# Two weight sums moved from VectorE to GpSimd, and a weight split issued one tile earlier, in a decoder layer's feed-forward part

## The reference

```python
def conv_ffn(h, prefix, w_up, conv_w, conv_b, w_down):
    up = h @ w_up                                        # 1024 -> 2 x 2816
    c, new_state = causal_dwconv(up, prefix, conv_w, conv_b)   # 3 taps along the tokens
    g, u = c[..., :D_FF], c[..., D_FF:]
    return (jax.nn.silu(g) * u) @ w_down, new_state      # 2816 -> 1024
```

## Time and profile before

| | |
|---|---|
| median of 3 runs | 877.42 us (877.25 to 877.79) |
| the profiled execution | 876.97 us, of which the span of the trace is 875.1 |
| PE busy | 850.4 us, 97% of the span |
| DVE busy | 554.5 us, 63% |
| ACT busy | 363.6 us, 42% |
| POOL busy | 68.8 us, 8% |
| granted TensorE clock, mean | 0.996 |
| the feed-forward part | from about 470 us to the end |

### The profile page before, as it was taken

One profiled execution on the slowest core, in us unless ns is written; L12 is line 12 of the kernel. 1 busy time (PEld: TensorE's weight loads), 2 busy tenths in 40 slices (PEclk: granted clock), 3 DMA queues, 4 the chain that ended last, 5 costly groups with the idle time before them and its releaser, 6 DMA issues.

```text
span 875.1 us, 17354 instructions
## 1 busy us (share of the span) xinstructions
PE 850.4 (97%) x6884; PEld 799.7 (91%) x6884; DVE 554.5 (63%) x981; ACT 363.6 (42%) x652; POOL 68.8 (8%) x149
## 2 busy tenths in 40 slices
PE   7999999999999999999999999999999999999995
PEld 7988878789999999877999999999999999999994
DVE  6344246677584732465455998778678696786754
ACT  7302133465553611354343754335244343452452
POOL 2320000000000000000000320100001001010200
PEclk9999999999999999999999999999999999999998
DMA  8798698731234555598233322232223322332222
GB/s 306 262 364 292 218 323 315 240 98 49 55 98 136 166 206 187 169 359 315 65 94 124 98 61 73 85 121 73 85 73 109 98 79 79 108 88 63 88 73 103
DMA packets 50146, 131.25 MB, mean 150 GB/s; under 512 B 5939, under 2 KB 8503, under 8 KB 49810
## 3 DMA queue, kind: packets, MB, share of 16 engines
q1 hardware_dynamic: 48064, 124.40, 43.1%
q0 software_dynamic: 1712, 5.62, 1.8%
q10 hardware_dynamic: 290, 0.12, 0.1%
HBM read 123.12 MB, written 7.00 MB: 149 GB/s over the span
## 4 chain that ended last, share of the span: by engine, by line
PE 69%; DVE 9%; ACT 4%; issue 3%; DVEq 0%; ACTq 0%
PE proj L1177 41%; PE proj L1133 3%; PE proj L1194 2%; PE proj L1196 2%; PE proj L1195 2%; DVE w_lo L1864 2%; PE score L1428 2%; PE score L1261 1%; PE score L1259 1%; PE score L1260 1%; PE T L1261 1%; PE T L1260 1%; PE T L1259 1%; PE score L1394 1%; DVE conv L2027 1%
## 5 line engine op out<-in xcount | busy, mean ns | idle before, releaser
L1177 PE MATMUL proj<-a_hi,w_hi 128*128 128x272 f32 (+1 forms) x740 | 160.7, 292 | 12.6 <-DVE w_lo L1864 6.3
L1528 ACT ACTIVATE w_hi<-w_raw 128x1024 fp32r<-128x1024 f32 (+2 forms) x128 | 119.0, 931 | 109.2 <-PE proj L1177 79.7
L1864 DVE TENSOR_TENSOR w_lo<-w_raw,w_hi 128x1024 fp32r<-128x1024 f32 (+2 forms) x128 | 136.9, 1070 | 34.7 <-ACT w_hi L1528 34.5
L1177 PE MATMUL proj<-a_lo,w_hi 128*128 128x272 f32 (+1 forms) x740 | 158.2, 288 | 0.0
L1177 PE MATMUL proj<-a_hi,w_lo 128*128 128x272 f32 (+1 forms) x740 | 158.0, 288 | 0.0
L1177 PEld LDWEIGHTS proj<-a_hi,w_hi 128*128 128x128 f32 x740 | 118.5, 189 | 20.9 <-DVE w_lo L1864 8.0
L1177 PEld LDWEIGHTS proj<-a_lo,w_hi 128*128 128x128 f32 x740 | 118.8, 189 | 0.0
L1177 PEld LDWEIGHTS proj<-a_hi,w_lo 128*128 128x128 f32 x740 | 118.4, 189 | 0.0
L1177 PE MATMUL proj<-d_hi,w_hi 128*128 128x272 f32 x448 | 92.4, 287 | 0.0
L1177 PE MATMUL proj<-d_lo,w_hi 128*128 128x272 f32 x448 | 92.1, 287 | 0.0
L1177 PE MATMUL proj<-d_hi,w_lo 128*128 128x272 f32 x448 | 92.1, 288 | 0.0
(11 more groups left out here) (360 smaller groups left out, 1653.0 us busy)
## 6 DMA issues: line engine op xcount, KB each, us to landing
w_raw<-in_w_up SPq DMA_DIRECT2D x28, 512.0 KB, 3.6
w_raw<-in_w_in SPq DMA_DIRECT2D x21, 512.0 KB, 3.9
early_pages<-in_cache_k SPq DMA_DIRECT2D x32, 256.0 KB, 6.2
pages<-in_cache_v SPq DMA_DIRECT2D x32, 256.0 KB, 5.3
c_pages<-in_cache_mem_k SPq DMA_DIRECT2D x16, 512.0 KB, 6.7
c_pages<-in_cache_mem_v SPq DMA_DIRECT2D x16, 512.0 KB, 5.8
p_raw<-in_w_up SPq DMA_DIRECT2D x16, 512.0 KB, 3.9
w_raw<-in_w_down SPq DMA_DIRECT2D x32, 256.0 KB, 2.6
```

The costliest lines, as they stand in the source:

```text
L1177: mm = pe.matmul(tile_banks(n)[:, half, 0:width], wt, act[:, at, half * HALF:half * HALF + width], start=(k == 0 and a == 0), stop=(k == w ...
L1528: act.activation(w_hi[:, n % W_HI_RING, 0:kt, :], w_raw[:, n % W_RING, 0:kt, :], ACT.Copy).then_inc(w_hi_ready, 1)
L1864: dve.tensor_tensor(w_lo[:, n % W_RING, 0:kt, :], w_raw[:, n % W_RING, 0:kt, :], w_hi[:, n % W_HI_RING, 0:kt, :].bitcast(F32), ALU.subtrac ...
```

## The change

Three edits. (1) In a plain column ahead of a paired one that has down tiles beside it, the splits of tile f + 3 (`w_hi` and `w_lo`) are issued in the step of the gate tile, right behind those of f + 2, and none in the step of the up tile. (2) GpSimd computes b12 - b11 and b22 - b12, with a wait of its own between the two. (3) DVE waits for both and computes the other two sums.

```diff
@@ make_schedule
         soon = PAIRED.index(i + 1) if i + 1 in PAIRED else None
         if not second and i == 0:
             s.append(("norm", "up"))
+        if soon is not None and beside_of(i):
+            after_hi, after_lo = split_next(f + 1)
+            hi, lo = ([], []) if second else (hi + after_hi, lo + after_lo)
         s += hi + [("up_in", i, int(second))] + lo
@@ the walk of GpSimd
+                if kind == "sums":
+                    for j in range(2):
+                        pool.wait_ge(sem(f"slot_landed1_{j}"), 16 * (PAGE_AREA.count(1) + arg + 1))
+                    if arg:
+                        wait_product(pool, arg - 1, 4)
+                    else:
+                        pool.wait_ge(sem("blend_lo"), 4)
+                    b11, b12, b22 = p_raw[:, 0, 0:4, :], p_raw[:, 1, 0:4, :], p_raw[:, 1, 4:8, :]
+                    pool.tensor_tensor(t_raw[:, 0, :, :], b12, b11, ALU.subtract).then_inc(sem("pool_sums"), 1)
+                    pool.wait_ge(sem("pool_sums"), 2 * arg + 1)
+                    pool.tensor_tensor(b12, b22, b12, ALU.subtract).then_inc(sem("pool_sums"), 1)
@@ the walk of VectorE, "sums"
                     one, two = slice(0, 4), slice(4, 8)
-                    b11, b21, b12, b22 = (p_raw[:, j, ks, :] for j in range(2) for ks in (one, two))
-                    side(dve.tensor_tensor(t_raw[:, 0, :, :], b12, b11, ALU.subtract))
-                    settle()
-                    side(dve.tensor_tensor(b12, b22, b12, ALU.subtract))
+                    b21, b22 = p_raw[:, 0, two, :], p_raw[:, 1, two, :]
+                    dve.wait_ge(sem("pool_sums"), 2 * arg + 2)
                     done(dve.tensor_tensor(t_raw[:, 1, :, :], t_raw[:, 0, :, :], b22, ALU.subtract))
                     dve.tensor_tensor(t_raw[:, 2, :, :], t_raw[:, 1, :, :], b21, ALU.add).then_inc(sem("sums_made"), 1)
```

## The result

| | before | after |
|---|---|---|
| median | 877.61 us of 4 runs (877.25 to 878.59) | 871.21 us of 4 runs (870.24 to 872.45) |
| ratio, 95% interval | | 0.992 (0.9907 to 0.9934) |
| the profiled execution, and its span | 876.97, 875.1 | 872.45, 870.7 |
| POOL busy | 68.8 us | 103.7 us |

The change is 0.8% faster, 6.4 us by the medians. I had forecast 877.3; the time lies just under my range. Two executions further down, one of the kernel before (1191.19 us) and one with pair 0's sums on VectorE (927.27 us), ran at a lower granted clock, and the ratios leave them out.

A forecast was written before the change was run, and what follows sets the result against it. The PE, busy 97% of the span, was taken as the bound, with 8.5 us of stalls to regain. Terms -5.6 + 3.6 + 1.9 = -0.1 on 876.97 gave 876.9, as a median 877.3 us; range 871.5 to 881.5.

The forecast's parts named there:

- the seven: PE stalls for w_lo at the second down tile of plain columns ahead of paired ones: 0.96 us each, 6.75 in all.
- The library load of 7.0 us: Column 4, ahead of GpSimd's first sum: a program library load, 6.3 plus 0.7 of issue; ends 0.3 and 10.
- the +3.6 of the wait: Column 4: VectorE waits for GpSimd behind the load, so the PE loses 5.4 us in place of 1.73.
- the +1.9 of the clock: Column 4: after a 5.3 us PE stop the clock falls to 1.2 GHz, about 19 matmuls 0.10 us longer.
- the rival of the cheap load: Column 4: library already there or in under 4 us; put at 872.4 us, chance 0.33.
- free form: Column 4, cheap load at no cost: stall 1.4 us, total -5.9, 871.5 us.
- -5.6 for seven pairs: Seven steady pairs: gain 0.8 us each, a 0.16 stall at the first down tile in place of 0.96.
- 1.2 us a sum: GpSimd's time per sum in the steady pairs, two streams and the fixed part; ends 0.5 and 1.6.
- the rival's 2.3 us stop: Column 4, cheap load of 3.9 us: the PE stands still 2.3 us, too short for the clock; total -5.0.
- no blocking: Steady pairs: GpSimd's sums don't block VectorE; the seven give 6.75, total 876.2 us, within the forecast's range.
- slow sums: Steady pairs: sums of 1.6 us each or more blocking, seven pairs give nothing; +5.5, 882.9 us, chance 0.09.
- the steady period of 276 matmuls: Sign in the steady pairs: about 34.7 us, 0.8 less than the 35.5 between two stalls before.

The follow-up runs named there:

- the split alone: Only the early split (w_hi and w_lo) put on the kernel before, all four sums on VectorE: 869.68 us, ratio 0.991.
- The two probes: The changed kernel plus two scratch GpSimd subtractions, at the program's start (871.77 us) or in column 4 ahead of pair 0's sums (869.84 us); one run each.
- the run with a sum twice: The changed kernel with GpSimd making the first sum two times in the seven steady pairs: 876.55 us, ratio 0.9974.
- the kernel with GpSimd's sums alone: The two GpSimd sums put on the kernel before, without the early split: 878.7 us, ratio 1.0009.
- the run with ScalarE's half alone: The early split for w_hi only on the kernel before; w_lo stays where it was, all sums on VectorE: 872.05 us, ratio 0.993.

## Why the prediction was wrong

- **That the PE's stalls are all that there is to gain, and that the early split takes all of the seven** was right: the split alone makes the stretch 8.12 us shorter, 6.75 + (1.73 - 0.31) = 8.17 by the stalls.
- **The library load of 7.0 us was the step that failed**, and with it the +3.6 of the wait and the +1.9 of the clock. I priced an operation that no row showed by GpSimd's transfers, because I took a load for a transfer and those were the rows at hand. The two probes show at most 0.1 us, below even my lower end of 0.3, so neither term was there to pay. The wait that I drew behind it was there in kind: VectorE does stand 1.28 us waiting for GpSimd in column 4, but the sum had begun 1.92 us late for another reason, and the PE lost 1.28 us instead of 5.4. This is the rival of the cheap load in its free form, which I put at 871.5, with 0.33 for the rival; 871.2 was measured. Its stall of 1.4 in column 4 was near the 1.28 measured. That the total fits is partly luck: its sum was -5.9, the stretch gave -6.96, and only what lies ahead of the stretch, which no run here explains, brings the medians back to -6.4. The Trainium skill (GPSIMD Engine Reference, "Instruction dispatch") has about 6 us for the first call to a freshly loaded kernel. No such time shows in the traces, neither at 2.1 us into the program nor at 525; since no run tells whether the library was still there from an execution before, that doesn't settle it against the page.
- **I had shown the first sum's condition, in the order of GpSimd's row, and not followed it.** It waits for `blend_lo` too, which is raised by VectorE's `e_lo`, and so it started 1.92 us behind the gate tile's copy; a load of up to that length would have been hidden.
- **The size of what the two engines do to each other was off.** I had VectorE 0.23 us later in a steady pair and a stall of 0.16, and so -5.6 for seven pairs; it is 0.11 earlier, six pairs have no stall, and the 0.19 in column 8 has its pause in column 7 behind it. The seven give 6.75 - 0.19 = 6.56. I took 1.2 us a sum as the time for which VectorE is shut out. The record of a sum lasts 1.29, yet the tap that was due at 663.54 ends 0.30 late, so it began at 663.84, 1.09 behind the sum's start; and the second sum, free to go at the first tap's end, 664.64, lets the second tap go at 666.40 - 0.80 = 665.60, 0.96 later. So it was 1.22 late instead of 1.55. That the exclusion works in both directions, and that sum two goes ahead of tap two, was as computed, and the run with a sum twice bears it out. The Trainium skill (SBUF — State Buffer, "SBUF: two separate sides") has the lock held for the whole instruction; the taps held up here agree with a lock and not with sharing, but VectorE is let in up to 0.2 us ahead of the end that GpSimd's record shows. The profile calls GpSimd's spans rough, so that may be the record's and not the lock's.
- **The clock.** The +1.9 as the price of a 5.3 us stop was near: 1.50 was measured with a stop of 5.25. But I had priced the rival's 2.3 us stop as free of it, by the earlier trace rows, and the profiled execution of the kernel with GpSimd's sums alone loses 1.53 us that way behind a stop of 2.57. It didn't bear on the result, since after stands still for 1.28 only and its clock stays at full.
- **Of the rivals**, "no blocking" falls by the taps of 1.72 and the run with a sum twice, and "slow sums" by the records of 1.29; the steady period of 276 matmuls that I gave as about 34.7 us is 34.54 (676.91 - 642.37, and the same in five of the seven; 34.73 where the 0.19 lies, 34.55 in the first), 0.93 less than before and not 0.8.

With the load at nothing and the seven pairs at the full 6.75, my sum would have been -6.75 - 0.45 = -7.2, 870.2 as a median, 1.0 below the one measured.

**A better version.** Both parts of what beats the two kernels are already among the runs: the early split alone, 869.68, and the split with GpSimd's sums in the seven steady pairs only, 869.70. They can't be told apart, and the first is the simpler. Against after they save the 1.16 us of the stretch, 0.97 in column 4 and 0.19 in column 8. The medians differ by 1.5, but were taken beside different runs of the kernel before, and the intervals of the ratios overlap.

## What to carry to other kernels

When an operation appears in no row, a row that only sounds like it is no price for it: GpSimd's transfers took 6.3 us, the load that I priced by them at most 0.1. If the ends of the bound are 0.3 and 10 us and the sum turns on it, the two ends are two forecasts. What else the instruction waits for, here 1.9 us for another engine, says how much of a load could show at all. Work moved from VectorE to GpSimd is not off VectorE's path where both read SBUF at the same time: here 1.22 of 1.32 us came back as longer taps, and where the first sum started late the move cost a wait. Look for a stall's cause in what order an idle engine takes its work: moving one 0.6 us operation of ScalarE ahead of two larger ones gave 5.7 of the 8.1 us.

## What the runs showed of the hardware

- The instruction that the build puts ahead of GpSimd's first `tensor_tensor`, MODIFY_POOL_CONFIG in the trace, cost under 0.1 us, at the start of the program and in the middle: two records of 1 to 11 ns, and the next instruction 0.05 to 0.09 us behind the one ahead of the load. Whether the library had stayed loaded from an execution before, no run here tells.
- A subtraction of two 128x512 f32 operands on GpSimd took 1.29 us; the same on VectorE 0.69. Where both wanted to run and read SBUF, one waited for the other: taps of 0.80 became 1.72, a gating of 0.69 became 1.60, a sum of 1.29 became 1.68 to 1.70 while the tap already under way kept its 0.79.
- TensorE's granted clock fell from full to half (2.4 to 1.2 GHz) behind a stop of 2.4 us between records, when the PE had already been back at work for 0.6 us, and the matmuls up to its rise took 1.53 us more; that is one profiled execution. Behind a stop of 5.1 us it was at half when the PE came back, and cost 1.50. A stop of 1.46 us before the change and of 1.04 after it left the clock alone.
- Short stalls are missing from the list of the PE's waits: the eight of the run with ScalarE's half alone, by the start times 0.36 us each and 0.26 in column 4, show only in the weight loads' list, and the 0.19 us of after's column 8 in neither.
